# Later and split steps of the attention units, later weight sums, and two more matmuls ahead of router steps in a hybrid decoder layer

## The chip, the cores and the metric

The kernel runs on one core of a Trainium2 chip, in one launch. The metric is the device time of that core in microseconds (us), the median of the runs shown. Inputs, weights and outputs are float32.

## What is computed

One layer for 256 prompt tokens and 8 sample tokens (264 rows, `NT`), model width 1024:

```python
proj = rmsnorm(x) @ w_in                    # xin | Bg | Cg | q | k | v | g_conv | g_attn
y_conv = Bg * causal_depthwise_conv3(Cg * xin)
y_attn = sliding-window GQA(q, k, v), window 128, T5 bias, one sink per head
x = x + (sigmoid(g_conv) * y_conv + sigmoid(g_attn) * y_attn) @ w_out
x = x + MoE(rmsnorm(x))                     # top-4 of 32 experts, clamped SwiGLU
```

The expert weights are 32 x 12.6 MB. Every expert is loaded and computed, in 16 pairs.

## The kernel before

**Stages.** The kernel is written as one program for each engine, with semaphores between them. Three stages follow each other on TensorE (PE): the input projection with the attention (`STEPS`), the output projection with the router (`BRANCH`), and the experts (`pair`). SyncE (SP) issues nearly all weight loads in one queue, in program order, into a ring of six slots and later into four units of two slots; each load waits until PE has begun or finished what was in its place.

**Input projection.** `w_in` comes in 13 chunks (c = 0 to 12) of 512 columns. Of most chunks PE computes four tiles of 128 columns, numbered 0 to 49 over the whole stage; chunk 7 holds tiles 26 to 29 (Cg), chunk 8 tiles 30 to 33 (xin). Chunks 6, 9, 10, 11 and 12 (`SEVEN`) are computed in seven products of half blocks instead of eight, a Strassen form: `slot(c, s)` is product s of chunk c, in `product()` on PE and `seven()` on VectorE (DVE). It needs sums of weights, four DVE instructions for each chunk (`add_weights`, placed by `SUM_STEPS`), and differences of the activations (`sides`, placed by `SIDE_STEPS`). DVE reads the products out of PSUM as r1, w, c22, c12 and c21; ScalarE (ACT) copies the first as t1 and computes the gates' sigmoids in place. PE's product s = 2 waits for t1, s = 6 for c22, and s = 0, 1, 4, 5 of the next chunk for the reads of the one before.

**Attention.** It is done in four units of 4 x 2 heads (`UNITS`): units 0 and 3 are of the first 128 queries, units 1 and 2 of the last 128 and have keys in two blocks. A unit goes through seven steps, whose places among the tiles and slots are in `UNIT_STEPS`: scores (PE), bias and peak (DVE), exp (ACT: eight activations, with a table load where the sigmoid's table was in), norm (for units 1 to 3 a reciprocal on DVE and then eight scalings on ACT), a move of 32 x 32 blocks by DMAs of 32 KB from the GpSimd (POOL) and SP queues into `stage[0]` (in `hn`) and `stage[1]` (`conv_row`), turn (DVE transposes them into `probT`), values (PE, then a DVE copy to `ya`). `plan()` puts each step behind its tile or slot; within one engine the steps stand in that order, and a step that has to wait holds up all that is behind it on that engine.

**What hangs on these steps.** SP issues the moves of units 1, 2 and 3 ahead of the loads of chunks 10, 12 and 13 (`MOVED_BEFORE`). After the loads of `w_out` (chunks 13 and 14) SP waits for the values of unit 3 (`FILL["values", 3]`), issues 12 moves of the expert biases, and then the first expert weights, in the order of `FIRST_ORDER`: pieces 0, 1, 11, 2, 3, 10, 7, 4, 5, 6, 8, 9 of 2 MB. POOL also waits for these values before its 12 moves. The biases are split on ACT and DVE into three bf16 parts (`split`, placed by `SPLIT_STEPS`). `conv_rows` (at `CONV_STEP`) is a DVE transposition; POOL stores its result with eight DMAs and then issues its moves of unit 3.

**Output and router.** `BRANCH` lists the steps for all engines. ("part", (n, k0, k1)) is the product of tokens 128 to 255 with half n of the last 512 columns of `w_out`, k from k0 to k1. ("x_cols", a) transposes new x on PE and copies it to `hT` on DVE (L1274), groups and logits are router products, count the ranks of the chosen experts, ahead the first two products of the last logits.

## Time and profile before

| | |
|---|---|
| runs, us | 1154.15, 1157.01, 1155.16 (median 1155.16) |
| profiled execution, us | 1155.1 |
| its span, us | 1153.2 |
| PE busy, us | 1100.5 (95%) |
| DVE / ACT / POOL busy, us | 440.8 / 183.7 / 82.8 |
| moved by DMA | 444.34 MB, mean 385 GB/s |
| granted TensorE clock | 0.993 of full speed |

The profile is of one execution. Times in the trace count from the start of the span, and 1.9 us of the execution lie outside it. An idle time in brackets is the time that the engine stood still before the instruction, with what released it. PE's instructions are counted twice in float32, since each is done in two passes.

### The profile page before, as it was taken

The page shows a single profiled execution, that of the slowest core. Times are in us where ns is not written, and L with a number is a line of the kernel's source. Part 1 is how long each engine was busy: PE and PEld are TensorE (multiplying, and loading weights), DVE is VectorE, ACT ScalarE, POOL GpSimd, SP SyncE. Part 2 cuts the span into 40 slices and gives each one's busy share as a digit, 9 for nine tenths or more (in the row PEclk, how much of TensorE's full clock was granted, in tenths as well). Part 3 has the DMA queues.
Part 4 walks back from the last instruction along what each step waited for, and adds up shares of the span by engine and source line. Part 5 has one row for each costly group of instructions (what it writes and reads, how often), then busy time and mean ns, then how long its engine had stood idle before and what let it go on. Part 6 is the DMA issues. An engine that isn't in the chain of part 4 may idle for free.

```text
span 1153.2 us, 14712 instructions
## 1 busy us (share of the span) xinstructions
PE 1100.5 (95%) x5895; PEld 494.2 (43%) x5895; DVE 440.8 (38%) x877; ACT 183.7 (16%) x388; POOL 82.8 (7%) x149
## 2 busy tenths in 40 slices
PE   9999999999999999999999999999999999999997
PEld 6678899453333333333333333333333333333332
DVE  4876775752353132332323232323232323232322
ACT  2123331220231111010101010101010101010101
POOL 1775033000000000000000000000000000000000
PEclk9999999999999999999999999999999999999999
DMA  9965439989999999999999999999999999999996
GB/s 318 327 194 130 151 98 300 399 317 431 424 419 426 421 430 429 435 432 430 429 435 433 431 429 435 433 429 431 435 432 429 432 434 432 429 433 434 425 423 280
DMA packets 52819, 444.34 MB, mean 385 GB/s; under 512 B 13036, under 2 KB 19596, under 8 KB 35868
## 3 DMA queue, kind: packets, MB, share of 16 engines
q1 hardware_dynamic: 46712, 436.13, 90.8%
q0 software_dynamic: 5216, 7.03, 2.4%
q10 hardware_dynamic: 852, 0.64, 0.2%
q8 instruction: 28, 0.46, 0.2%
q14 instruction: 11, 0.09, 0.0%
HBM read 439.78 MB, written 2.37 MB: 383 GB/s over the span
## 4 chain that ended last, share of the span: by engine, by line
PE 54%; DMA 38%; POOL 3%; DVE 3%; ACT 1%; issue 1%; SPq 0%; DVEq 0%; ACTq 0%; POOLq 0%
PE pA L1960 29%; DMA ring<-in_w_up 21%; PE pB L1960 18%; DMA ring<-in_w_down 10%; PE pM L1960 6%; DMA area<-in_w_up 5%; PE pM L1963 1%; DMA hn<-in_cache_v_win 1%; POOL keys L952 1%; DMA ring<-in_w_in 1%; PE pA L1963 1%; DMA out<-area 0%; POOL out L960 0%; POOL area L931 0%; POOL conv_row L937 0%
## 5 line engine op out<-in xcount | busy, mean ns | idle before, releaser
L1960 PE MATMUL pA<-ring,hn 128*64 128x512 f32 x1536 | 352.6, 602 | 23.4 <-DMA ring<-in_w_up 23.4
L1960 PEld LDWEIGHTS pA<-ring,hn 128*64 128x64 f32 x1536 | 105.3, 137 | 219.2 <-issue 185.5
L1960 PE MATMUL pB<-ring,area 128*64 128x512 f32 (+2 forms) x784 | 171.5, 591 | 6.6 <-DMA ring<-in_w_down 5.8
L1960 PE MATMUL pB<-area,ring 128*128 128x264 f32 (+2 forms) x928 | 148.5, 350 | 2.2 <-ACT tmp L1080 0.8
L1960 PEld LDWEIGHTS pB<-area,ring 128*128 128x128 f32 (+1 forms) x928 | 120.4, 175 | 27.7 <-issue 4.3
L1960 PE MATMUL pA<-area,hn 128*64 128x512 f32 x512 | 119.3, 609 | 10.4 <-DMA area<-in_w_up 10.4
L1960 PEld LDWEIGHTS pB<-ring,area 128*64 128x64 f32 (+2 forms) x784 | 58.6, 136 | 101.2 <-issue 87.8
L1812 DVE TENSOR_TENSOR x<-pM,x 128x512 f32<-128x512 f32 x60 | 40.1, 692 | 147.3 <-PE pM L1960 147.2
L1183 ACT ACTIVATE area<-area 128x512 f32<-128x512 f32 x30 | 18.9, 631 | 385.2 <-DVE area L1795 385.2
L1727 DVE COPY conv_row<-pM 128x512 f32<-128x512 f32 x30 | 20.6, 686 | 146.4 <-PE pM L1960 146.4
L1960 PEld LDWEIGHTS pA<-area,hn 128*64 128x64 f32 x512 | 36.1, 140 | 74.6 <-issue 59.8
L1960 PE MATMUL pB<-area 128*64 128x512 f32 (+2 forms) x300 | 66.4, 547 | 1.2 <-DVE area L1260 1.2
L1795 DVE TENSOR_SCALAR area<-pA 128x512 f32<-128x512 f32 x30 | 20.7, 691 | 92.6 <-PE pA L1960 92.6
L1960 PE MATMUL pM<-area 128*128 128x512 bf16 (+2 forms) x368 | 52.4, 330 | 1.5 <-DVE x L1812 1.4
L1730 DVE TENSOR_TENSOR hn<-pM,fnorm 128x512 f32<-128x512 f32 x30 | 20.7, 691 | 84.9 <-PE pM L1963 84.5
L1837 DVE COPY area<-pB 64x512 f32<-64x512 f32 x15 | 10.4, 694 | 101.5 <-PE pB L1960 101.5
L1960 PEld LDWEIGHTS pM<-area 128*128 128x128 bf16 (+2 forms) x368 | 18.7, 96 | 52.4 <-issue 35.6
L1960 PE MATMUL pM<-hn,x 128*128 128x512 bf16 (+1 forms) x120 | 37.4, 396 | 0.0
L1960 PEld LDWEIGHTS pB<-area 128*64 128x64 f32 (+2 forms) x300 | 20.7, 130 | 35.0 <-issue 30.3
L1195 ACT ACTIVATE area<-pA 128x512 f32<-128x512 f32 x15 | 9.0, 597 | 120.7 <-PE pA L1963 120.7
L1963 PEld LDWEIGHTS pA<-cst,area 128*128 128x128 f32 x120 | 16.8, 210 | 24.3 <-issue 24.3
L1191 ACT ACTIVATE area<-pA 128x512 f32<-128x512 f32 x15 | 8.9, 596 | 107.0 <-PE pA L1963 107.0
(335 smaller groups left out, 933.9 us busy)
## 6 DMA issues: line engine op xcount, KB each, us to landing
ring<-in_w_up SPq DMA_DIRECT2D x36, 4096.0 KB, 29.8
ring<-in_w_down SPq DMA_DIRECT2D x18, 4096.0 KB, 29.1
area<-in_w_up SPq DMA_DIRECT2D x12, 4096.0 KB, 30.2
ring<-in_w_up SPq DMA_DIRECT2D x17, 2048.0 KB, 14.6
area<-in_w_down SPq DMA_DIRECT2D x6, 4096.0 KB, 30.0
ring<-in_w_in SPq DMA_DIRECT2D x22, 1024.0 KB, 11.2
ring<-in_w_up SPq DMA_DIRECT2D x14, 1024.0 KB, 9.3
ring<-in_w_down SPq DMA_DIRECT2D x13, 1024.0 KB, 25.9
```

Of the source, the lines that this page charges most:

```text
L952: pool.dma_start(v_row[32 * a:32 * a + 32, 0:2, 32 * q:32 * q + 32], v_blocks[32 * q:32 * q + 32].rearrange("p (m a r) -> p m a r", m=2, a ...
L1183: nc.scalar.activation(early_sig if kind == "first" else sig[:, e, :], early_glu if kind == "first" else glu[:, e, :], ACT.Sigmoid, scale= ...
L1191: nc.scalar.activation(turned, pA[:, 0:512], ACT.Copy).then_inc(aT_ready, 1)
L1195: nc.scalar.activation(turned, pA[:, 1024:1536], ACT.Copy).then_inc(aT_ready, 1)
L1727: return V.tensor_copy(xrow[:, 512 * half:512 * half + 512], b)
L1730: return V.tensor_tensor(xsT[:, 4 * half:4 * half + 4, :], b.rearrange("p (k s) -> p k s", k=4), fw[:, 4 * half:4 * half + 4, :], ALU.mult)
L1795: V.tensor_scalar(gl, u[:, 0, e], LIMIT, None, ALU.min).then_inc(glu_ready, 1)
L1812: V.tensor_tensor(xo, bank(k), xo, ALU.add).then_inc(misc_free, 1)
L1837: V.tensor_copy(y_pair[64:128, 512:1024], pB[64:128, 1, :]).then_inc(y_ready_dve, 1)
L1960: return pe.matmul(out, w, m, start=start, stop=stop, skip_group_check=True)
L1963: return pe.transpose(out, src, ident[0:src.shape[0], 0:src.shape[0]])
```

## The change

Four tables are changed.

- `UNIT_STEPS`: exp and norm of unit 1 stand one tile earlier, its turn four steps earlier and its values one tile earlier. Bias, peak and exp of unit 2 stand one tile earlier, its turn and values one slot later. Unit 3's turn goes from slot (10, 6) to (11, 1), its values from (11, 1) to (11, 3).
- The turn of units 1 and 2 is split: the transposition of `stage[0]` stays at the turn, that of `stage[1]` stands at a step of its own (`SECOND_TURNS`).
- `SUM_STEPS` of chunks 9 and 10, the last of `SIDE_STEPS`, `SPLIT_STEPS` and `CONV_STEP` are placed anew. Since the last side is now computed behind slot (9, 0), chunk 9 uses `side3[0]` like chunk 6, and only the chunks in `AFTER_XIN` (10, 11, 12) use `side3[1]`.
- `BRANCH`: one more k of part 0 ahead of groups, and one more k of part 1 ahead of count 0.

The diff also adds a case for a Cg chunk in the seven-product form. `SEVEN` holds no such chunk, so this case adds no instruction; it is left out below.

```diff
-UNIT_STEPS = [(11, 12, 12, 13, 13, 18, 19), (18, 18, 19, 20, 21, 27, 28),
-              (26, 27, 28, 29, 30, slot(9, 2), slot(9, 4)),
-              (slot(9, 3), slot(9, 4), slot(9, 5), slot(10, 0), slot(10, 2), slot(10, 6), slot(11, 1))]
-SPLIT_STEPS = [slot(9, 4), slot(9, 6), slot(10, 1)]
-CONV_STEP = slot(10, 1)
-SIDE_STEPS = [20, 21, slot(6, 2), slot(6, 3), 33]
-SUM_STEPS = {6: (19, 20, slot(6, 0), slot(6, 1)), 9: (slot(6, 5), 26, 26, 28), 10: (29, 29, 30, 31),
+UNIT_STEPS = [(11, 12, 12, 13, 13, 18, 19),
+              (18, 18, 19, 19, 20, slot(6, 5), 27),
+              (26, 26, 27, 28, 30, slot(9, 3), slot(9, 5)),
+              (slot(9, 3), slot(9, 4), slot(9, 5), slot(10, 0), slot(10, 2), slot(11, 1), slot(11, 3))]
+SECOND_TURNS = (26, slot(9, 3))
+SPLIT_STEPS = [slot(9, 6), slot(10, 1), slot(10, 4)]
+CONV_STEP = slot(10, 2)
+SIDE_STEPS = [20, 21, slot(6, 2), slot(6, 3), slot(9, 0)]
+SUM_STEPS = {6: (19, 20, slot(6, 0), slot(6, 1)),
+             9: (slot(6, 4), 27, 28, 29),
+             10: (30, 31, slot(9, 0), slot(9, 1)),
              11: (slot(10, 0), slot(10, 1), slot(10, 3), slot(10, 4)),
              12: (slot(11, 2), slot(11, 3), slot(12, 1), slot(12, 2))}
...
+    for n, step in enumerate(SECOND_TURNS):
+        after[step].append(("turn", len(UNITS) + 1 + n))
...
+          ("s_split", 0), ("out", (1, 0)), ("x_cols", 2), ("rms", 0), ("part", (0, 0, 6)), ("groups", 0), ("x_cols", 3),
+          ("logits", 0), ("part", (0, 6, KT)), ("half", 0), ("part", (1, 0, 4)), ("count", 0), ("part", (1, 4, 6)),
...
-            gated = TILES[2 + 4 * (c - 1)][0] != "bg"
+            kind = TILES[2 + 4 * (c - 1)][0]
+            gated = kind in ("gc", "ga")
-                if name != "c11" or not gated:
+                if name != "c11" or kind == "bg":
-                if name == "t1" or gated:
+                if name == "t1" or gated or name == "c11" and kind == "cg":
...
+AFTER_XIN = [c for c in SEVEN if STEPS.index(("slot", (c, 0))) > STEPS.index(("sides", 4))]
...
-                elif what == "turn":
+                elif what == "turn" and a < len(UNITS):
                     dve.wait_ge(prob_moved, MOVED[a])
                     if SYNC_MOVED[a]:
                         dve.wait_ge(moved_by_sync, SYNC_MOVED[a])
-                    for b in range(UNITS[a][0] + 1):
-                        ins = V.transpose(probT[:, b].rearrange("p h q -> p (h q)"), stage[b])
-                    ins.then_inc(probT_ready, 1)
+                    ins = V.transpose(probT[:, 0].rearrange("p h q -> p (h q)"), stage[0])
+                    if UNITS[a][0] == 0:
+                        ins.then_inc(probT_ready, 1)
+                elif what == "turn":
+                    V.transpose(probT[:, 1].rearrange("p h q -> p (h q)"), stage[1]).then_inc(probT_ready, 1)
...
-                                  (s1, side1, bank_y, False), (s3, side3[c > SEVEN[0]], bank_u, True), (s4, b22, bank_v, True),
+                                  (s1, side1, bank_y, False), (s3, side3[c in AFTER_XIN], bank_u, True), (s4, b22, bank_v, True),
...
-                    pe.wait_ge(h_ready, KT + (3 if c == SEVEN[0] else 5))
-                    if opening:
+                    pe.wait_ge(h_ready, KT + (5 if c in AFTER_XIN else 3))
+                    if UNITS_BEFORE[c]:
                         pe.wait_ge(prob_biased, UNITS_BEFORE[c])
-                    else:
+                    if not opening:
```

**The norm of unit 1.** On DVE, around the last two tiles of chunk 5 (`area<-pB 128x264`), before. The two `stat` rows are the norm of unit 1 (wait `exp_done`), the `ring` rows weight sums of chunk 6, the `128x528` rows sides.

```order
L1384 TENSOR_TENSOR area<-area 128x528
L1371 TENSOR_TENSOR ring<-ring 128x1024 [waits sums_ready]
L1453 TENSOR_TENSOR area<-pB,area 128x264 [waits tile_full]
L1384 TENSOR_TENSOR area<-area 128x528 [waits h_ready]
L1541 TENSOR_TENSOR stat<-stat 128x8 [waits exp_done]
L1543 RECIPROCAL stat<-stat 128x8 [waits dve_step]
L1371 TENSOR_TENSOR ring<-ring 128x1024
L1312 TENSOR_TENSOR tmp<-tmp,pB 128x264 [waits tile_free_act,tile_full]
```

And in the changed kernel:

```order
L1401 TENSOR_TENSOR area<-area 128x528
L1388 TENSOR_TENSOR ring<-ring 128x1024 [waits sums_ready]
L1558 TENSOR_TENSOR stat<-stat 128x8 [waits exp_done]
L1560 RECIPROCAL stat<-stat 128x8 [waits dve_step]
L1470 TENSOR_TENSOR area<-pB,area 128x264 [waits tile_full]
L1401 TENSOR_TENSOR area<-area 128x528 [waits h_ready]
L1388 TENSOR_TENSOR ring<-ring 128x1024
L1324 TENSOR_TENSOR tmp<-tmp,pB 128x264 [waits tile_free_act,tile_full]
```

The norm now stands ahead of the read of tile 21, behind the sums of step 20, where it stood behind that read and a side.

**The turn of unit 3.** On DVE, end of chunk 10 and start of chunk 11, before. `STREAM_TRANSPOSE` is the turn, `area<-pM` the copy of the values, `tmp` and `rt` from `pB` are r1 and w of chunk 11, the `ring` rows sums of chunk 12.

```order
L1555 STREAM_TRANSPOSE area<-hn 128x1024 [waits moved_by_sync,prob_moved]
L1298 TENSOR_TENSOR area<-tmp,area 128x2x132 [waits tile_free_dve,tile_free_act]
L1312 TENSOR_TENSOR tmp<-tmp,pB 128x264 [waits sig_used,tile_free_act,tile_full]
L1561 COPY area<-pM 128x2x2x128 [waits misc_full]
L1371 TENSOR_TENSOR ring<-ring 128x1024 [waits ring_free,ring_full2]
L1312 TENSOR_TENSOR rt<-tmp,pB 128x264 [waits tile_full]
L1371 TENSOR_TENSOR ring<-ring 128x1024 [waits sums_ready]
```

And in the changed kernel:

```order
L1309 TENSOR_TENSOR area<-tmp,area 128x2x132 [waits tile_free_dve,tile_free_act]
L1324 TENSOR_TENSOR tmp<-tmp,pB 128x264 [waits sig_used,tile_free_act,tile_full]
L1571 STREAM_TRANSPOSE area<-hn 128x1024 [waits moved_by_sync,prob_moved]
L1388 TENSOR_TENSOR ring<-ring 128x1024 [waits ring_free,ring_full2]
L1324 TENSOR_TENSOR rt<-tmp,pB 128x264 [waits tile_full]
L1388 TENSOR_TENSOR ring<-ring 128x1024 [waits sums_ready]
L1580 COPY area<-pM 128x2x2x128 [waits misc_full]
```

The turn is behind the last gate of chunk 10 and r1 of chunk 11, and the copy of the values is behind w and two sums instead of ahead of them.

**The router steps.** On PE, from the first part of half 0 to the transposition of x_cols 4, before. The rows from `ring,area` with `128x256` are the parts, `32x128` is groups, `mask` is count 0.

```order
L1960 MATMUL pA<-ring,area 128x256 x5
L1960 MATMUL pM<-area,router 32x128 [waits wr_ready,misc_free]
L1960 MATMUL pM<-area,router 32x128 x7
L1963 MATMUL pM<-cst,x 128x128 [waits x_added,misc_free]
L1963 MATMUL pM<-cst,x 128x128 x3
L1960 MATMUL pM<-cst,sprobT 128x32 [waits misc_free]
L1960 MATMUL pA<-ring,area 128x256 x3
L1960 MATMUL pB<-ring,area 128x256 x3
L1960 MATMUL pM<-mask,router 8x32 [waits mask_ready,misc_free]
L1960 MATMUL pM<-mask,router 128x32 x2
L1960 MATMUL pB<-ring,area 128x256 x3
L1963 MATMUL pM<-cst,x 128x128 [waits x_added,misc_free]
L1963 MATMUL pM<-cst,x 128x128
```

And in the changed kernel:

```order
L1979 MATMUL pA<-ring,area 128x256 x6
L1979 MATMUL pM<-area,router 32x128 [waits wr_ready,misc_free]
L1979 MATMUL pM<-area,router 32x128 x7
L1982 MATMUL pM<-cst,x 128x128 [waits x_added,misc_free]
L1982 MATMUL pM<-cst,x 128x128 x3
L1979 MATMUL pM<-cst,sprobT 128x32 [waits misc_free]
L1979 MATMUL pA<-ring,area 128x256 x2
L1979 MATMUL pB<-ring,area 128x256 x4
L1979 MATMUL pM<-mask,router 8x32 [waits mask_ready,misc_free]
L1979 MATMUL pM<-mask,router 128x32 x2
L1979 MATMUL pB<-ring,area 128x256 x2
```

Six matmuls instead of five stand ahead of groups, and two instead of three behind count 0.

## Rows read from the trace of the kernel before

**Rows 1.** Busy time by stretch; columns as in the second line.
```profile
core 0: us, PE busy (x) PEld busy (x) DVE busy (x) ACT busy (x) POOL busy (x), PEclk, DMA share, GB/s
75.00:210.00 135.00, 133.65 (x1054) 115.74 (x1055) 95.66 (x198) 34.66 (x110) 41.51 (x74) 1.00 0.57 178
210.00:247.00 37.00, 35.72 (x177) 22.14 (x177) 23.61 (x78) 12.12 (x27) 0.00 (x0) 1.00 0.84 342
247.00:512.00 265.00, 262.35 (x1280) 93.58 (x1278) 88.31 (x180) 41.01 (x64) 0.00 (x0) 1.00 1.00 424
512.00:1136.00 624.00, 584.39 (x2827) 209.90 (x2827) 180.40 (x308) 73.30 (x120) 0.00 (x0) 0.99 1.00 431
```

**Rows 2.** PE in order of time: start, length, idle before.
```profile
105.82 3.87 PE L1960 MATMUL pB<-area,ring 128*128 128x132 f32 x32 [0.82 <-ACT tmp L1080]
...
118.58 1.32 PE L1960 MATMUL pA<-keys,area 64*32 64x160 f32 x64
...
179.47 1.08 PE L1960 MATMUL pM<-area,keys 128*64 128x256 f32 x8 [0.22 <-issue]
...
228.96 2.32 PE L1960 MATMUL pA<-ring,area 128*128 128x256 f32 x10
...
231.67 0.65 PE L1960 MATMUL pM<-area,router 128*32 128x128 f32 x16 [0.38 <-DVE area L1274]
```

**Rows 3.** ScalarE in order of time, 95 to 169 us.
```profile
95.55 0.43 ACT L1095 ACTIVATE area<-area,stat 128x160 f32<-128x160 f32 x1 [22.21 <-DVE stat L1536]
...
98.85 0.19 ACT L1097 ACTIVATE stat<-stat 128x8 f32<-128x8 f32 x1
...
102.83 2.66 ACT L1102 ACTIVATE area<-area,stat 128x160 f32<-128x160 f32 x8 [3.79 <-DVE stat L1543]
...
133.29 1.28 ACT L1095 ACT_TABLE_LOAD   x1
...
168.36 0.62 ACT L1110 ACTIVATE conv_row<-hn 128x512 bf16<-128x512 f32 x1
```

**Rows 4.** VectorE in order of time.
```profile
99.14 1.22 DVE L1371 TENSOR_TENSOR ring<-ring 128x1024 f32<-128x1024 f32 x1
...
121.32 1.52 DVE L1521 SCALAR_TENSOR_TENSOR area<-pA,area 128x640 f32<-128x640 f32 x2
...
178.13 1.25 DVE L1555 STREAM_TRANSPOSE area<-hn 128x1024 f32<-128x1024 f32 x1 [1.32 <-DMA hn<-area]
...
230.89 0.68 DVE L1274 COPY area<-pM 128x512 f32<-128x512 f32 x1
```

**Rows 5.** GpSimd's DMA issues in order of time.
```profile
169.18 0.59 POOL L991 DMA_DIRECT2D out<-hn  x1 [19.79 <-DVE hn L1598]
...
173.68 2.91 POOL L971 DMA_DIRECT2D hn<-area  x5
```

**Rows 6.** SyncE's DMA issues in order of time.
```profile
176.64 2.36 SPq L740 DMA_DIRECT2D ring<-in_w_out  x4
...
181.32 0.87 SPq L747 DMA_DIRECT2D keys<-conv_row  x1
...
190.16 1.05 SPq L821 DMA_DIRECT2D ring<-in_w_up  x2
...
228.83 10.35 SPq L821 DMA_DIRECT2D ring<-in_w_up  x2
```

**Rows 7.** The two gaps of the DMA engines; columns as in rows 1.
```profile
228.00:231.00 3.00, 3.00 (x16) 2.29 (x14) 2.92 (x6) 0.00 (x0) 0.00 (x0) 1.00 0.50 131
...
235.00:239.00 4.00, 4.00 (x23) 3.18 (x22) 2.64 (x13) 0.51 (x2) 0.00 (x0) 1.00 0.03 12
```

**Rows 8.** DMA issues from 160 to 262 us: KB each, median us to landing.
```profile
keys<-conv_row SPq DMA_DIRECT2D x6, 32.0 KB, 8.5
...
keys<-conv_row POOLq DMA_DIRECT2D x6, 32.0 KB, 5.7
...
hn<-area POOLq DMA_DIRECT2D x5, 32.0 KB, 1.9
```

More of the change, by code:

```diff
@@ L248 @@
 BRANCH = [("out", (2, 0)), ("out", (0, 0)), ("x_cols", 0), ("rms", 2), ("out", (0, 1)), ("x_cols", 1), ("logits", 2),
-          ("s_split", 0), ("out", (1, 0)), ("x_cols", 2), ("rms", 0), ("part", (0, 0, 5)), ("groups", 0), ("x_cols", 3),
-          ("logits", 0), ("part", (0, 5, KT)), ("half", 0), ("part", (1, 0, 3)), ("count", 0), ("part", (1, 3, 6)),
+          ("s_split", 0), ("out", (1, 0)), ("x_cols", 2), ("rms", 0), ("part", (0, 0, 6)), ("groups", 0), ("x_cols", 3),
+          ("logits", 0), ("part", (0, 6, KT)), ("half", 0), ("part", (1, 0, 4)), ("count", 0), ("part", (1, 4, 6)),
           ("x_cols", 4), ("part", (1, 6, KT)), ("half", 1), ("ahead", 1), ("x_cols", 5), ("rms", 1), ("logits", 1),
@@ L1080, in _ @@
                         nc.scalar.activation(t1, pairs_of(bank_x), ACT.Copy).then_inc(tile_free_act, 1)
+                    elif s == 2 and (c, "c11") in ACT_DONE and not gated:
+                        act.wait_ge(tile_full, FULL[c, 2])
+                        nc.scalar.activation(quarter(cx[:, :, 2:], c, "c11"), pairs_of(bank_x), ACT.Copy).then_inc(tile_free_act, 1)
                     elif s == 2 and gated:
@@ L1309, in seven, with place_of @@
                 gated = (c, "c22") in ACT_DONE
+                plain = TILES[2 + 4 * (c - 1)][0] == "cg"
                 def read(name, out, a, b):
                     V.tensor_tensor(out, a, pairs_of(b), ALU.add).then_inc(tile_free_dve, 1)
+                def place_of(name, g):
+                    return quarter(cx[:, :, 2:], c, name) if plain else g
                 def times(name, g):
+                    if plain:
+                        return
                     dve.wait_ge(tile_free_dve, DVE_READ[c, name])
@@ L1322, in seven @@
                     return
-                if s != 2 or not gated:
+                if s != 2 or not (gated or plain):
                     dve.wait_ge(tile_full, FULL[c, s])
@@ L1329, in seven @@
                     read("r1", r1, t1, bank_y)
-                elif s == 2 and not gated:
+                elif s == 2 and not (gated or plain):
                     out = quarter(yc, c, "c11")
@@ L1336, in seven @@
                     dve.wait_ge(tile_free_dve, DVE_READ[c, "w"])
-                    read("c22", c_, w_, bank_u)
+                    read("c22", place_of("c22", c_), w_, bank_u)
                     if not gated:
@@ L1340, in seven @@
                 elif s == 5:
-                    read("c12", w_, w_, bank_v)
+                    read("c12", place_of("c12", w_), w_, bank_v)
                     if gated:
@@ L1348, in seven @@
                         finish(c, "c12")
-                    read("c21", r1, r1, bank_u)
+                    read("c21", place_of("c21", r1), r1, bank_u)
                     if not gated:
```

## The prediction

> **What bounds the kernel now.** I read the busy time by stretch first, since PE is busy for 95% of the span and that figure alone tells nothing. Up to 210 us PE stands still for 135.00 - 133.65 = 1.4 us after 75 us while the DMA engines are busy for 0.57 of the time; from 210 to 247 us it stands still for another 1.3 us. From 512 us on it is the other way round: PE is idle for 40 of 624 us and the DMA share is 1.00 [rows 1]. Between 247 and 512 us both are full. So the end is set by the stream of expert weights, at about 430 GB/s, and that stream starts when PE frees its places. A microsecond saved ahead of 247 us reaches the end only if it lets that stream go on earlier; a microsecond by which an issue of SP slips costs only if the stream has no gap left to swallow it.
>
> The gaps are in the windows of the stream: a half-idle stretch from 228 to 231 us, and one with a share of 0.03 from 235 to 239 us [rows 7]. Together they are 1.5 + 3.9 = **5.4 us** of idle DMA time. Both end when PE has got far enough in the router: SP issues the next pieces at 228.83 us and then ten microseconds later [rows 6].
>
> Then I read PE in order of time, for its idle before an instruction, and from there to the engine named. Three places lie where the change works [rows 2]: 0.82 us ahead of product s = 2 of chunk 6 (waiting for t1 on ACT), 0.22 us ahead of the values of unit 3, and 0.38 us ahead of groups (waiting for DVE's copy of x_cols 2). All of PE's idle time from 75 to 247 us is 2.6 us, so nothing that the change does there can bring more than that. PE's work stays the same, matmul for matmul.
>
> **The change part by part.**
>
> *Norm of unit 1, one tile earlier.* Its exps end at 98.85 + 0.19 = 99.0 us [rows 3]. In the new order the norm stands behind a weight sum that ends at 100.3 us [rows 4], and no longer behind the read of tile 21. Reciprocal and its companion need some 0.3 us, so the eight scalings (2.66 us) start at about 100.7 us instead of 102.83 and end at 103.3 instead of 105.5. Product s = 0 of chunk 6 ends about 1.8 us before 105.0, where PE became ready, thus at 103.2 (a slot takes 3.7 / 2 = 1.8 us [rows 2]). t1 is then written by 103.8, and PE needs it at 105.0. The whole **0.82 us** goes. What is late next is r1 for s = 3, which follows on time.
>
> *Turn and values of unit 1.* The moves now start at 103.4 us. Ten on SP take 6.8 us to issue at the 0.6 to 0.7 us each that its other rows show, the last lands about 2 us later [rows 8], so near 112.3. The turn stands behind slot (6, 5), at 113.2. If it had to wait, c21 would be read later, and PE needs that only ahead of the scores of unit 2, at 118.58 - 0.8 = 117.8 us [rows 2]: cover of over 2 us. The second transposition follows bias 2, so 119.1 + 1.5 + 1.2 = 121.8 us [rows 4], and PE asks for it one tile (3.6 us) behind the end of these scores at 119.1, at 122.7. Cost nothing, with 0.9 us in hand.
>
> *Exp of unit 2 ahead of the copy of tile 29 on ACT.* Table load 1.28, exps 3.5, two copies 0.8 [rows 3]: 5.6 us behind the end of tile 28. PE wants that bank for tile 31, two tiles or 7.2 us behind it. Nothing, with 1.6 us in hand.
>
> *Sums and the last side.* The same instructions, on DVE, which is 0.71 busy [rows 1]. Sums of chunk 10 end behind slot (9, 1), a whole chunk ahead of use. Nothing.
>
> *Splits and conv_rows.* The second cast now runs on ACT behind the exps of unit 3, where the third ran at 168.36 us [rows 3]. With PE 0.8 us earlier that cast ends at 168.5. DVE then subtracts (about 1.0 us, two instructions of the cast's shapes), does the norm of unit 3 and transposes. POOL's stores therefore start at about 170.6 instead of 169.18 us [rows 5], its moves of unit 3 at 175.1 instead of 173.68, and these are issued by 178.1. Behind the waiting subtraction stand w and c22 of chunk 10; PE needs c22 at about 172.9 us and has it at 172.1. Nothing on PE, but a margin of 0.8 us.
>
> *Turn and values of unit 3, later.* Before, DVE waited 1.32 us for the moves and PE 0.22 us for the turn [rows 4, 2]. Now PE has two more slots to do: it comes to the values at 179.25 - 0.82 + 3.6 = 182.05 us. The moves land at 179.5 (the last issued at 177.5, plus 1.9 [rows 8]) and the turn is done at 180.8. So the **0.22 us** goes too. The copy of the values now follows w and two sums; it ends at about 184.3, where it ended at 181.3. SP's bias moves (8.8 us of issuing), and behind them the expert weights, start **3.0 us later**: at 193.2 instead of 190.16 us [rows 6]. The stream before was unbroken from there to 228 us, so its first seven pieces now end at about 231.2. The piece issued at 228.83 - 1.2 us then ends at 236.1, and the next is issued, with PE earlier by 1.4, at 237.4. The 5.4 us of gap shrink by 3.0 + 1.4 to 1.0 us. Cost nothing while that is left; beyond it each microsecond counts in full.
>
> *Router.* Five matmuls take 2.32 us, one 0.46 [rows 2]. The sixth covers the 0.38 us of waiting (DVE's copy, at 230.89 us [rows 4], hangs on a chain that moves with PE). Groups start 0.08 us later than they could, but 0.46 us less of part work stands behind count 0, whose other inputs move with PE. From there to the last logits the path is shorter by **0.38 us**.
>
> Sum: 0.82 + 0.22 + 0.38 = 1.42 us, passed on to the stream because its later pieces are gated by PE. The profiled execution took 1155.1 us (span 1153.2 and 1.9 around it), 0.06 below the median, so the forecast is 1155.1 - 1.4 = **1153.7 us**. Bounds of the sum: all of PE's idle time gone, -2.6 us; nothing gained, 0.
>
> **The rivals.**
>
> *A: the moves of unit 3 land late.* On POOL they are now issued until 178.1 us, while SP, freed 0.8 us earlier, issues `w_out` from 175.8 us on. Before, POOL was done at 176.6, when `w_out` began [rows 5, 6]. In the quiet such a move lands in 1.9 us, beside heavy loads one of 32 KB took 5.7 us on POOL and 8.5 on SP [rows 8]. At 5.7 the last lands at 183.2, the turn is done at 184.5, and PE stands still for 2.5 us; SP's issue slips by 6.5 us, which the gap of 5.4 + 2.5 - 1.4 just swallows. The time is 1155.1 - 1.4 + 2.5 = 1156.2 us, slower than before. At 8.5 it would be 1159.0. It decides from a landing above 3.1 us. For it: the two queues now overlap by 2 us. Against it: the loads of `w_out` moved few bytes in their first 2 us. The Trainium skill ("DMA: Bandwidth & Descriptors", section "Queues, rings and completion order") says that each DMA engine takes turns between the queues at packet granularity, and that a completion write lands only after every earlier write of that engine, whichever queue it is from. By that rule the late case is the natural one, for a move issued behind bulk work; no run here shows it for these moves.
>
> *B: the saving does not reach the stream.* If the copy of the values slips by 1 us more than I reckon, the gap is gone and PE's 1.4 us are eaten by waits later: 1155.1 us, no change. For it: only 1.0 us is left. Against it: the window before was measured, not guessed.
>
> *C: a wait takes the place of t1's.* One of the margins of 0.8 or 0.9 us (c22 of chunk 10, second turn of unit 1) is not there, and PE loses up to 1 us: 1154.7.
>
> A gain over 0.3% would need 3.5 us, more than PE's idle time there.
>
> **How the numbers follow.** Forecast 0.52, A 0.25 (of it 0.06 beyond 1158.6), B 0.13, C 0.10. A measurement tells a difference from none from about 0.3%, 3.5 us. All but the end of A lies within; for the spread of the runs (1154.15 to 1157.01) I leave 0.06 for faster. Range: below the forecast 1.2 us for the rest of the idle time and 0.5 for the spread, 1152.0; above, A at 5.7 us and 0.7 for the spread, 1156.9.
>
> **What would show it.** In the changed profile: no idle ahead of s = 2 of chunk 6, of the values of unit 3, and of groups; SP's first expert piece at about 193 us; a DMA gap before 239 us of about 1 us in place of 5.4; pair 0's first matmul 1.4 us earlier. A DVE wait at the turn of unit 3 of over 2 us with PE idle behind it means A; a DMA share of 1.00 through 225 to 240 us means B. I am wrong if PE's idle time from 75 to 247 us grows.

## The result, and the profile after

| | before | changed |
|---|---|---|
| runs side by side, us | 1155.6 median of 13 (1154.15 to 1157.01) | 1159.3 median of 13 (1155.86 to 1161.56) |
| ratio | | 1.003, 95% interval 1.0022 to 1.0039 |
| profiled execution, its span, us | 1155.1, 1153.2 | 1158.37, 1156.3 |

The forecast was 1153.7 us. The changed kernel is slower, by 3.7 us in the medians, and its runs spread over 5.7 us where those of before spread over 2.9. The time lies above the range, and past the 1156.2 us of rival A, near its far end of 1159.0.

Where the time went is seen first in the windows of the changed kernel (the columns are those of [rows 1]).

```profile
core 0: us, PE busy (x) PEld busy (x) DVE busy (x) ACT busy (x) POOL busy (x), PEclk, DMA share, GB/s
75.00:210.00 135.00, 131.90 (x1047) 115.25 (x1048) 92.61 (x194) 33.99 (x109) 41.52 (x74) 0.99 0.51 163
210.00:247.00 37.00, 36.28 (x172) 21.81 (x172) 25.04 (x78) 12.00 (x25) 0.00 (x0) 1.00 0.89 367
```

Up to 210 us PE now stands still for 135.00 - 131.90 = 3.1 us, against 1.4 [rows 1]; with the 0.7 us up to 247 it is 3.8 against 2.6. That is the sign named beforehand ("I am wrong if PE's idle time from 75 to 247 us grows"). PE in order of time shows that two of the three waits of [rows 2] are gone and the third has grown:

```profile
99.79 8.92 PE L1979 MATMUL pB<-area,ring 128*128 128x264 f32 x71
...
117.60 1.32 PE L1979 MATMUL pA<-keys,area 64*32 64x160 f32 x64
...
184.69 1.98 PE L1979 MATMUL pM<-area,keys 128*64 128x256 f32 x8 [2.81 <-issue]
186.59 4.39 PE L1979 MATMUL pA<-area,ring 128*128 128x132 f32 x32
...
234.69 0.65 PE L1979 MATMUL pM<-area,router 128*32 128x128 f32 x16
...
249.42 2.80 PE L1979 MATMUL pA<-ring,hn 128*64 128x512 f32 x12
```

The product that followed 0.82 us of idle runs on without a stop (99.79 to 108.7 is one row), and groups at 234.69 has no idle time before it. But PE stands still for 2.81 us ahead of the values of unit 3, where it was 0.22. The view names no releaser there (`issue`); the turn that PE needs ends at 183.34 + 1.25 = 184.6 us by VectorE's row further down, 0.1 us before PE goes on. The values themselves then take 1.98 us instead of 1.08, and the first two products behind them 4.39 instead of 3.87 us. The windows of this stretch tell why (the granted clock is the third number from the end):

```profile
183.00:185.00 2.00, 0.31 (x2) 0.32 (x4) 1.66 (x2) 0.00 (x0) 0.00 (x0) 0.82 1.04 384
185.00:187.00 2.00, 2.00 (x10) 0.94 (x7) 2.00 (x3) 0.00 (x0) 0.00 (x0) 0.50 1.06 389
187.00:189.00 2.00, 2.00 (x16) 2.00 (x16) 0.77 (x2) 0.00 (x0) 0.94 (x2) 0.83 1.05 386
```

The granted clock was 0.50 from 185 to 187 us, that is 1.2 in place of 2.4 GHz, right behind the 2.81 us in which PE did nothing. Before, it was 1.00 throughout this stage [rows 1].

From PE I went to VectorE, which does the norm and the turns, and from there to the moves: four views of the changed kernel, VectorE, POOL's and SP's issues in order of time, and the DMA issues from 160 to 262 us with KB each and the median us to landing.

```profile
100.59 0.20 DVE L1560 RECIPROCAL stat<-stat 128x8 f32<-128x8 f32 x1
...
120.62 1.25 DVE L1575 STREAM_TRANSPOSE area<-conv_row 128x1024 f32<-128x1024 f32 x1
...
183.34 1.25 DVE L1571 STREAM_TRANSPOSE area<-hn 128x1024 f32<-128x1024 f32 x1 [4.60 <-DMA hn<-area]
```

```profile
170.28 0.59 POOL L999 DMA_DIRECT2D out<-hn  x1 [21.87 <-DVE hn L1617]
...
174.78 2.91 POOL L979 DMA_DIRECT2D hn<-area  x5
```

```profile
175.67 2.54 SPq L748 DMA_DIRECT2D ring<-in_w_out  x4
```

```profile
hn<-area SPq DMA_DIRECT2D x5, 32.0 KB, 2.0
hn<-area POOLq DMA_DIRECT2D x5, 32.0 KB, 4.8
...
out<-hn POOLq DMA_DIRECT2D x4, 8.0 KB, 1.8
```

POOL's stores and moves are issued as forecast (170.28 and 174.78 us; 170.6 and 175.1 were reckoned), the last move starts at about 177.1 and is issued by 177.7. But the median landing of POOL's five is 4.8 us, where it was 1.9 [rows 8], and the turn waits 4.60 us, until 183.34. SP's five, issued just before `w_out`, land in 2.0. Between the two stands one event: at 175.67 SP begins to issue `w_out`. Its bytes come later, as two windows of the changed kernel show (the last number is GB/s):

```profile
177.00:178.00 1.00, 1.00 (x11) 1.00 (x10) 0.00 (x0) 0.00 (x0) 0.69 (x2) 1.00 0.31 43
178.00:179.00 1.00, 1.00 (x11) 1.00 (x10) 0.43 (x1) 0.00 (x0) 0.00 (x0) 1.00 1.02 387
```

PE's first matmul of the experts starts at 249.42 us. Before, in the same place of the program, it was

```profile
246.84 3.65 PE L1960 MATMUL pA<-ring,hn 128*64 128x512 f32 x16
```

Of the 3.27 us between the profiled executions 2.58 are there at that point; the rest is within the spread of the runs. The profiled execution of the changed kernel, 1158.37 us, lies 0.9 below its median, so it holds only part of the loss of 3.7.

### The profile page after: what moved, and what is told of

It is laid out like the page before. It is cut to its first block, busy times and chain, and to the rows that moved or that the text cites. A ratio compares the mean times of both kernels' runs of the same rounds, so it can differ in the third digit from the quotient of the medians.

```text
span 1156.3 us, 14714 instructions
## 1 busy us (share of the span) xinstructions
PE 1102.3 (95%) x5895; PEld 495.1 (43%) x5895; DVE 440.7 (38%) x877; ACT 183.3 (16%) x388; POOL 82.8 (7%) x149
## 4 chain that ended last, share of the span: by engine, by line
PE 55%; DMA 38%; POOL 3%; DVE 2%; ACT 1%; issue 1%; SPq 0%; DVEq 0%; ACTq 0%; POOLq 0%
PE pA L1979 29%; PE pB L1979 19%; DMA ring<-in_w_up 16%; DMA ring<-in_w_down 12%; DMA area<-in_w_up 8%; PE pM L1979 6%; PE pM L1982 1%; DMA hn<-in_cache_v_win 1%; POOL keys L960 1%; DMA ring<-in_w_in 1%; PE pA L1982 1%; DMA out<-area 0%; POOL out L968 0%; POOL area L939 0%; POOL conv_row L945 0%
```

## The experiments

Two theories stood against each other. **L**: the moves of unit 3 land late because `w_out` is under way beside them, and the loss is PE's idle time, with the slow clock behind it. **S**: the loss comes from SP's slip, since the stream of expert weights starts later. Every kernel ran in turn with the kernel before on one chip, and each ratio is against it.

### 1. The moves ahead of the stores

```diff
             move_blocks(2)
+            move_blocks(3)
             pool.wait_ge(blocks_turned, CONV_TURNED)
             for q in range(4):
...
-            move_blocks(3)
```

> The changed kernel, but POOL issues its five moves of unit 3 ahead of the eight stores of conv_rows. Theory L (the moves of unit 3 land late because POOL issues them beside the load of w_out, and PE loses its idle time and then its clock): the last POOL move is issued near 175 us and lands within about 2 us; no DVE wait of over 0.5 us at the turn of unit 3, no PE idle ahead of the values of unit 3, granted clock 1.00 there, first expert matmul near 245.5 us; time 1.2 to 1.6 us below the kernel before, near 1154.2. Rival S (the later start of the expert stream is the cost, 3.0 us of it by the place of the values alone): SP's first expert piece still comes near 193 us and the time stays within 1 us of the changed kernel, near 1158.5.

**Measured: 1153.86 us** (1152.62 to 1155.25, 11 runs), ratio 0.9986 (0.9977 to 0.9995). DMA issues from 160 to 262 us (KB each, median us to landing), then PE in order of time:

```profile
hn<-area POOLq DMA_DIRECT2D x5, 32.0 KB, 1.9
...
out<-hn POOLq DMA_DIRECT2D x4, 8.0 KB, 5.7
```

```profile
181.78 1.08 PE L1979 MATMUL pM<-area,keys 128*64 128x256 f32 x8
182.79 3.87 PE L1979 MATMUL pA<-area,ring 128*128 128x132 f32 x32
...
245.11 3.65 PE L1979 MATMUL pA<-ring,hn 128*64 128x512 f32 x16
```

The two landings show L in the plainest way. The five moves, now issued from 172.60 us, land in 1.9 us; the stores, now issued last and beside `w_out`, land late in their place: those of 8 KB in 5.7 us, where they took 1.8. Nobody waits for them. In these runs moves and stores alike land late when POOL issues them behind the first load of `w_out`. PE has no idle time ahead of the values, they take 1.08 us again, and the experts' first matmul comes at 245.11, 1.73 us earlier than before and 4.31 earlier than in the changed kernel.

### 2. conv_rows and the splits earlier

```diff
-SPLIT_STEPS = [slot(9, 6), slot(10, 1), slot(10, 4)]
-CONV_STEP = slot(10, 2)
+SPLIT_STEPS = [slot(9, 5), slot(9, 6), slot(10, 1)]
+CONV_STEP = slot(10, 1)
```

> The changed kernel with the splits at (9, 5), (9, 6), (10, 1) and conv_rows at (10, 1), so that POOL's stores and its moves of unit 3 come about 2 us earlier while the order on POOL stays. Theory L: POOL's last move is issued near 175.5 us, lands before 178, no PE idle ahead of the values; time as moves_first, near 1154.2. Rival S: near 1158.5. If the long landing were of the moves themselves and not of the overlap with w_out, the DVE wait at the turn stays above 3 us here and in moves_first.

**Measured: 1153.32 us** (1152.85 to 1154.73, 11 runs), ratio 0.9981 (0.9972 to 0.9990). The moves are issued from 173.40 us and land in 1.8; PE does not stop at the values.

### 3. w_out held back

```diff
                 if c in MOVED_BEFORE:
                     move_blocks(MOVED_BEFORE[c])
+                if c == W_IN_CHUNKS:
+                    sp.wait_ge(prob_moved, MOVED[3])
                 if before(c):
                     sp.wait_ge(ring_free, before(c))
```

The wait stands in SP's loop over the chunks, ahead of the loads of chunk 13, the first of `w_out`.

> The changed kernel with one more wait on SP: the load of w_out is issued only when POOL's moves of unit 3 have landed. Theory L: these moves land 2 us after their issue (1.7 to 2.3) although POOL issues them as late as in the changed kernel, until about 177.7; landing near 179.5, DVE's wait at the turn about 1 us, no PE idle ahead of the values; w_out starts 4 us later and is still there before PE needs it near 201 us; the expert stream starts near 193 us; time near 1154.5. If POOL's moves are slow by themselves: landing still 5 us and more, PE idle as in the changed kernel, time near 1159.

**Measured: 1153.67 us** (1152.9 to 1154.48, 11 runs), ratio 0.9982 (0.9973 to 0.9991). This one keeps POOL's order and times and takes only the bulk away. POOL's and SP's issues in order of time, and the landing:

```profile
174.72 2.90 POOL L981 DMA_DIRECT2D hn<-area  x5
```

```profile
178.87 2.14 SPq L750 DMA_DIRECT2D ring<-in_w_out  x4
```

```profile
hn<-area POOLq DMA_DIRECT2D x5, 32.0 KB, 1.8
```

Issued at 174.72 to 177.6, as late as in the changed kernel, the moves land in 1.8 us. So the cause is not the late issue in itself but the load beside it.

### 4. The kernel before, with conv_rows late

```diff
-SPLIT_STEPS = [slot(9, 4), slot(9, 6), slot(10, 1)]
-CONV_STEP = slot(10, 1)
+SPLIT_STEPS = [slot(9, 6), slot(10, 1), slot(10, 4)]
+CONV_STEP = slot(10, 2)
```

> The kernel before with only the places of the splits and of conv_rows changed to those of the change. Theory L: this part alone brings the loss. POOL's moves of unit 3 are issued until about 178 us, beside w_out (issued from 176.6); the turn, which here stands one slot earlier, waits 3 to 6 us on DVE, PE stands still 2 to 5 us ahead of a product of chunk 11 or the values, and its clock falls to half for some 2 to 3 us: time 1158 to 1162. Rival S: the turn and the values have the old places, so the stream starts late only by the wait; without a wait the time is that of the kernel before, 1155.6.

**Measured: 1164.05 us** (1163.12 to 1164.76, 5 runs), ratio 1.0075 (1.0061 to 1.0088). PE and VectorE of this kernel in order of time, and its windows:

```profile
185.04 1.98 PE L1960 MATMUL pM<-area,keys 128*64 128x256 f32 x8 [6.31 <-issue]
186.95 5.04 PE L1960 MATMUL pB<-area,ring 128*128 128x132 f32 x32
```

```profile
183.69 1.25 DVE L1555 STREAM_TRANSPOSE area<-hn 128x1024 f32<-128x1024 f32 x1 [7.41 <-DMA hn<-area]
```

```profile
183.00:185.00 2.00, 0.00 (x0) 0.00 (x0) 1.31 (x2) 0.00 (x0) 0.00 (x0) 0.50 1.05 369
...
187.00:189.00 2.00, 2.00 (x10) 2.00 (x10) 1.82 (x2) 0.00 (x0) 0.96 (x2) 0.50 1.09 395
189.00:193.00 4.00, 4.00 (x36) 4.00 (x35) 0.98 (x2) 0.39 (x1) 3.67 (x9) 0.95 0.47 146
```

The two-line edit alone makes the loss. Idle time grew by 6.31 - 0.22 = 6.1 us, and at half the clock the values and the two products behind them took (1.98 - 1.08) + (5.04 - 3.87) = 2.1 us more. Together 8.2, against 1164.05 - 1155.76 = 8.3 measured, above the 1158 to 1162 that I had expected. Profile against profile, PE comes to the experts 254.46 - 246.84 = 7.6 us later and the execution is 1163.12 - 1155.10 = 8.0 us longer. What PE loses here reaches the end nearly one for one.

### 5 and 6. Only the stream held back

```diff
             sp.wait_ge(misc_free, FILL["values", 3])
             sp.wait_ge(bias_cast, SPLITS)
+            sp.wait_ge(tile_full, FULL[11, 5])
```

This is the kernel of experiment 1 with one more wait on SP: in the first run, `stream_held`, for product 5 of chunk 11, in the second, `stream_held_longer`, for product 0 of chunk 12 (`FULL[12, 0]`).

> The kernel moves_first, and in addition SP waits for product s = 5 of chunk 11 ahead of the bias moves. PE has nothing more to wait for; the stream of expert weights alone is held back. In moves_first the copy of the values ended at 183.4 us and the first expert piece was issued at 191.98; product 5 ends at about 190.3, so that piece should be issued at about 199, 7 us later. Idle DMA time from 228 to 239 us in moves_first was 3.00 * 0.06 + 4.00 * 0.20 + 4.00 * 0.69 = 3.7 us. If a slip is swallowed by that gap and counts in full beyond it, 3.3 us are left over: 1153.9 + 3.3 = 1157.2 us, and no idle DMA time from 228 to 239 us. If the slip costs nothing because the later pieces are gated by PE: 1153.9. If it costs in full from the start: 1160.9.

> As stream_held, but SP waits for product s = 0 of chunk 12, which ends at about 190.1 us (a product takes 1.8 to 1.9 us). In stream_held the first expert piece was issued at 194.44 us, 2.46 later than in moves_first, and of the idle DMA time from 228 to 239 us 1.4 us (4.00 * 0.36) was left, at no cost in time. Now the piece should be issued at about 198.1, another 3.7 us later. If the gap swallows what it holds and the rest counts in full: 3.7 - 1.4 = 2.3 us, so 1153.8 + 2.3 = 1156.1 us, a DMA share near 1.00 from 228 to 239 us. If slips cost nothing: 1153.8.

**Measured: 1153.80 us** (1153.12 to 1154.91, 11 runs) and **1153.81 us** (1152.67 to 1154.57, 11 runs), both with the ratio 0.9985 (0.9976 to 0.9994). The first expectation had the end of product 5 wrong (186.4 and not 190.3 us, since a product takes half of what I took for it), so it tested a slip of 2.5 us; the second tested 198.09 - 191.98 = 6.1. SP's issues and the windows of the second kernel:

```profile
198.09 1.05 SPq L830 DMA_DIRECT2D ring<-in_w_up  x2
...
226.95 9.94 SPq L830 DMA_DIRECT2D ring<-in_w_up  x2
```

```profile
228.00:231.00 3.00, 3.00 (x30) 2.20 (x28) 2.33 (x8) 1.52 (x4) 0.00 (x0) 1.00 1.03 437
...
235.00:239.00 4.00, 3.78 (x28) 3.36 (x27) 2.52 (x12) 1.15 (x4) 0.00 (x0) 1.00 0.96 410
```

The first expert piece is issued at 198.09 us, 7.9 us later than before [rows 6], the gaps of [rows 7] are all but full, and the time is that of experiment 1. That is later than in the changed kernel itself:

```profile
196.45 1.05 SPq L829 DMA_DIRECT2D ring<-in_w_up  x2
```

So the slip of the stream doesn't make the loss. S is refuted for slips as long as this one, and with it the arithmetic by which 1.0 us was left. Part of the error is the unit: the DMA share counts an engine as busy while it moves little. In experiment 1 the windows read

```profile
228.00:231.00 3.00, 3.00 (x29) 2.24 (x27) 2.59 (x8) 0.93 (x4) 0.00 (x0) 1.00 0.94 322
231.00:235.00 4.00, 4.00 (x25) 3.24 (x23) 2.92 (x14) 1.65 (x3) 0.00 (x0) 1.00 0.80 336
235.00:239.00 4.00, 3.78 (x28) 3.34 (x27) 2.68 (x13) 0.71 (x3) 0.00 (x0) 1.00 0.31 66
```

By the shares 0.18 + 0.80 + 2.76 = 3.7 us are free there; by the bytes, against 430 GB/s, 0.8 + 0.9 + 3.4 = 5.0 us. The slip of 6.1 us is still 1 us longer than that, and what took up this last microsecond stays open. Where a slip begins to cost was not tried.

### 7. The values one product later

```diff
-              ... slot(10, 2), slot(11, 1), slot(11, 3))]
+              ... slot(10, 2), slot(11, 1), slot(11, 4))]
```

> The changed kernel with the values of unit 3 one product later still, behind slot (11, 4). The moves of unit 3 are issued as late as in the changed kernel, and should land as late (median near 4.8 us), but PE now does another product of 3.8 us ahead of the values, so it comes there at about 185.6 us, when the turn is done at 184.6. Theory L (all the loss is PE's idle time and the half clock behind it): no idle ahead of the values, granted clock 1.00, time 1153.9. Theory S (the late start of the stream costs too): first expert piece at about 197 us, 5 us later than in moves_first, against a gap of 3.7: 1153.9 + 1.3 = 1155.2.

**Measured: 1155.06 us** (1153.53 to 1156.23, 11 runs), ratio 0.9996 (0.9987 to 1.0005). A product takes 1.9 us, not the 3.8 that I had written, so the wait should shrink by 1.9 and not vanish. PE in order of time, and the landing:

```profile
183.89 1.08 PE L1979 MATMUL pM<-area,keys 128*64 128x256 f32 x8 [0.84 <-issue]
```

```profile
hn<-area POOLq DMA_DIRECT2D x5, 32.0 KB, 5.0
```

It shrank from 2.81 to 0.84 us, the moves landed as late as before (5.0), and after an idle time of 0.84 us the values took 1.08 us: the clock did not fall. The median is 1.2 us above experiment 1. The profiled execution, 1153.53 us, is the shortest of the eleven, so its 0.84 us do not measure what the others lost. The median lies near the 1155.2 that I had given to S, but the first expert piece came at 195.42 us here, and 198.09 cost nothing in experiment 6. That leaves PE's remaining wait as the likely reason; in the longer executions it was not traced.

### 8. The router steps alone, in the kernel before

```diff
-          ... ("part", (0, 0, 5)), ("groups", 0), ("x_cols", 3),
-          ("logits", 0), ("part", (0, 5, KT)), ("half", 0), ("part", (1, 0, 3)), ("count", 0), ("part", (1, 3, 6)),
+          ... ("part", (0, 0, 6)), ("groups", 0), ("x_cols", 3),
+          ("logits", 0), ("part", (0, 6, KT)), ("half", 0), ("part", (1, 0, 4)), ("count", 0), ("part", (1, 4, 6)),
```

> The kernel before with the new order of the router steps alone. The term of the sum says -0.38 us: no idle ahead of groups, 1155.8 - 0.4 = 1155.4. If the work moved there is missed behind count 0, a new idle time of up to 0.46 us stands there and the time is that of before, 1155.8.

**Measured: 1155.15 us** (1154.24 to 1155.85, 11 runs; the kernel before 1155.65 beside it), ratio 0.9994 (0.9985 to 1.0003). The medians differ by 0.5 us, the size of the term, but the interval takes in no change. In the trace the idle time ahead of groups is gone and no new one stands behind it.

### 9. Units 1 and 2 alone

The changed kernel with unit 3, the splits, `conv_rows` and the router steps as before:

```diff
-              (... slot(10, 0), slot(10, 2), slot(11, 1), slot(11, 3))]
+              (... slot(10, 0), slot(10, 2), slot(10, 6), slot(11, 1))]
-SPLIT_STEPS = [slot(9, 6), slot(10, 1), slot(10, 4)]
-CONV_STEP = slot(10, 2)
+SPLIT_STEPS = [slot(9, 4), slot(9, 6), slot(10, 1)]
+CONV_STEP = slot(10, 1)
```

> The changed kernel with unit 3, splits, conv_rows and the router steps as before: only the steps of units 1 and 2, the sums and the last side are new. The term of the sum says -0.82 us (no idle ahead of product s = 2 of chunk 6), 1155.8 - 0.8 = 1155.0; moves of unit 3 issued before w_out as in the kernel before, landing in about 1.9 us. PE comes to the values of unit 3 earlier by 0.8, so that part of the 0.82 can come back there as a wait where the chain of unit 3 hangs on POOL or ACT and not on PE: then 0.22 + 0.8 = 1.0 us of idle ahead of the values and 1155.8. If this part brought the loss, it would be over 1157.

**Measured: 1154.64 us** (1153.63 to 1154.84, 11 runs; before 1155.65), ratio 0.9990 (0.9981 to 0.9999). A gain of 1.0 us (0.1 to 2.2 by the interval) for a term of 0.82. PE's waits of this kernel between 95 and 235 us are one:

```profile
230.12 0.65 PE L1979 MATMUL pM<-area,router 128*32 128x128 f32 x16 [0.38 <-DVE area L1285]
```

It is the 0.38 us ahead of groups, which this kernel keeps. Nothing came back at the values of unit 3.

### 10. The idle time filled with work

```diff
                     o = misc_bank()
+                    if a == 3:
+                        for n in range(12):
+                            matmul(o[:, 0:HALF], weights(11)[0][:, n % K2, 0:128], b11[:, n % K2, :])
                     pe.wait_ge(probT_ready, a + 1)
```

> The changed kernel with 12 more matmuls of 128x132 on PE ahead of its wait for the turn of unit 3; their result is overwritten by the values. At 0.235 us each (3.76 us for 16) they fill 2.8 us, as long as PE stood still there in the profiled execution of the changed kernel. They change no transfer and nothing on VectorE. If the stretch at half the clock is brought about by the idle time: granted clock 1.00 from 183 to 189 us, the values 1.08 us again in place of 1.98 and the product behind them 3.76 in place of 4.39, so 1.5 us less: 1159.3 - 1.5 = 1157.8. If the clock fell for another cause: still 0.50 there and 1159.3. In both cases DVE still waits over 3 us for the moves.

**Measured: 1156.34 us** (1155.81 to 1158.10, 11 runs), ratio 1.0012 (1.0002 to 1.0021). PE in order of time, a window, and VectorE:

```profile
181.24 2.86 PE L1979 MATMUL pM<-area,ring 128*128 128x132 f32 x24
185.62 1.08 PE L1979 MATMUL pM<-area,keys 128*64 128x256 f32 x8 [1.52 <-DVE area L1571]
186.63 3.87 PE L1979 MATMUL pA<-area,ring 128*128 128x132 f32 x32
```

```profile
185.00:187.00 2.00, 1.38 (x11) 0.85 (x12) 2.00 (x4) 0.00 (x0) 0.00 (x0) 1.00 1.06 388
```

```profile
184.32 1.25 DVE L1571 STREAM_TRANSPOSE area<-hn 128x1024 f32<-128x1024 f32 x1 [6.05 <-DMA hn<-area]
```

The trace has two records for each float32 matmul, so x24 is the twelve. In this execution the moves landed later still (the turn waited 6.05 us), and PE spent 2.86 us on the filling and 1.52 idle. The clock stays at 1.00, the values take 1.08 and the products behind them 3.87 us. Part of the loss is thus the slow clock and not the wait. In the profiled execution of the changed kernel it cost (1.98 - 1.08) + (4.39 - 3.87) = 1.4 us. The two profiled executions themselves are only 0.3 us apart (1158.37 and 1158.10, here the longest of the eleven): PE began the values 0.9 us later, at 185.62 against 184.69. The medians, 1159.3 and 1156.34, differ by 3.0, twice the 1.4 and more than the 1.5 expected. The runs here stand in two groups, six from 1155.81 to 1156.34 and five from 1157.57 to 1158.10, as if the landing had two values, the earlier one hidden by the filling; that is a guess, since only one execution of each kernel was traced. How late the moves landed, and what the clock cost, in those executions of the changed kernel that took over 1160 us stays open too.

### 11 and 12. Both mendings together

The edit of experiment 2 on top of experiment 1, and on top of experiment 3.

> The changed kernel with both mendings: conv_rows and the splits at steps (9, 5), (9, 6), (10, 1), (10, 1), and the moves of unit 3 ahead of POOL's stores. Either alone took away all idle time ahead of the values (1153.86 and 1153.32), so the second should add nothing: 1153.3 to 1153.9, moves issued from about 170 us and landing in 1.9, SP's first expert piece at 191.9. If the earlier start of the stream were worth something, up to 0.6 us less than moves_first: 1153.2.

> The changed kernel with conv_rows and the splits early, and w_out held until the moves of unit 3 have landed. In conv_early these moves landed in 1.8 us with w_out beside them, so holding w_out should change nothing but its issue, at about 177.5 us in place of 175.7: 1153.3. If the spread of landing from run to run were left in conv_early, this kernel would be lower or spread less than 1152.85 to 1154.73.

**Measured: 1153.57 us** (1152.63 to 1155.07, 11 runs), ratio 0.9987 (0.9978 to 0.9996), and **1153.31 us** (1152.77 to 1153.96, 11 runs), ratio 0.9980 (0.9971 to 0.9989). As expected, once PE's wait is gone there is nothing left for a second mending. Only the issue was not as expected: with both mendings the moves start at 172.32 us and not at about 170, since POOL waits for unit 3's scalings on ACT. Experiment 2 changes only two lines and is 2.4 us below the kernel before, 6.0 below the changed one; the intervals do not tell it from experiments 1 and 3.

What the landings have in common, row by row (the first column of times runs from the start of the first issue to the end of the last; the clock is that of the values):

| kernel | POOL issues the moves | SP issues `w_out` from | landing, median us | clock behind |
|---|---|---|---|---|
| before | 173.68 to 176.6 | 176.64 | 1.9 | 1.00 |
| moves_first | 172.60 to 175.5 | 175.63 | 1.9 | 1.00 |
| conv_early | 173.40 to 176.3 | 176.26 | 1.8 | 1.00 |
| w_out_held | 174.72 to 177.6 | 178.87 | 1.8 | 1.00 |
| changed | 174.78 to 177.7 | 175.67 | 4.8 | 0.50 |
| before_conv_late | 175.21 to 178.1 | 176.10 | 4.8 | 0.50 |
| values_later | 174.13 to 177.0 | 175.02 | 5.0 | 1.00 |
| idle_filled | 174.31 to 177.2 | 175.19 | 4.8 | 1.00 |

In the kernel before, the last move was issued just as the first load of `w_out` began (176.6 and 176.64), and in `conv_early` too. Wherever POOL's issues ran on for 2.0 us beyond that, the moves landed late. Between these two cases nothing was tried, so how much overlap is harmless stays open.

## Why the prediction was wrong

**The step that failed** is in the part on unit 3: "The moves land at 179.5 (the last issued at 177.5, plus 1.9 [rows 8])". The issue was right to 0.4 us; the landing was a figure from the quiet, used for five moves of which three were now issued behind the first load of `w_out`. They landed at about 183.3. Experiments 1 and 3 show it from two sides, one by moving the moves, one by taking `w_out` away. The case stood there as rival A, with its rule, and I gave it 0.25. My reason against it was that `w_out` moved few bytes in its first 2 us. It was no reason: the last move, issued at 177.1, would have landed at 179.0 in the quiet, and the bulk of `w_out` was there from 178 us on (43 GB/s up to 178 us, 387 behind it). The Trainium skill ("DMA: Bandwidth & Descriptors", section "Queues, rings and completion order") says that an engine takes turns between queues and that a completion write lands only after every earlier write of that engine. The trace agrees with the effect (4.8 against 1.8 us, and the stores' 5.7 against 1.8 when they take the moves' place); which of the two parts of the rule does it no run here tells apart.

**A's price was too low.** At a landing of 5.7 us it reckoned 2.5 us of idle PE and 1156.2 us. The idle time was 2.81, but the half clock behind it had no term: 1.4 us in the profiled execution, 2.1 in experiment 4. Together PE came 4.3 us later to the experts than in experiment 1. The forecast had none of these 2.81 + 1.4 = 4.2 us; the median missed it by 5.6, and the 1.4 us between are not explained; 0.9 of them is what the median lies above the profiled execution. A's slip of SP's issue does not come out of its own terms either: 3.0 + 2.5 is 5.5 and not 6.5 us. That 196.45 - 190.16 = 6.3 were measured is luck.

**The three gains were right.** The 0.82 us went (experiment 9: 1.0 measured), the 0.38 too (experiment 8: 0.5, not certain), and with the moves in time the 0.22 as well. The kernels of the whole change in which the moves land in time took 1153.3 to 1153.9 us, about the forecast's 1153.7. In part that is luck: the kernel before took 1155.5 to 1155.8 beside them and not the 1155.1 from which I had reckoned, so they gained 1.7 to 2.4 us for a sum of 1.4. PE's gain in experiment 1 is 246.84 - 245.11 = 1.7 us.

**The margins held.** The turn of unit 1 went from step 27 to slot (6, 5), which is three steps and not four, and it did not wait. The reciprocal ahead of the scalings of unit 1 starts at 100.59 and they at 100.83 (100.7 us reckoned), the second transposition ends at 120.62 + 1.25 = 121.9 (121.8), and no wait took t1's place: C did not come.

**The margin of the stream was wrong in the other direction.** "Beyond it each microsecond counts in full" was stated for 1.0 us left of 5.4. A first piece 7.9 us later than before cost nothing (experiment 6). In the changed kernel itself, with its first piece at 196.45, the DMA share from 235 to 239 us was 0.82, so even there the gap was not used up. Rival B had its 0.13 from that arithmetic and was not there. What did reach the end was the time by which PE came late to the experts. Against the profile of before it is 7.6 us of 8.0 in experiment 4 and 2.6 of 3.3 in the changed kernel. The second is rough, since executions of one kernel differ by over 2 us: against experiment 1, whose profiled execution (1155.25) is the longest of its eleven, it is 4.3 us of PE for 3.1 in time.

## What to carry to other kernels

Take the landing time of a small transfer from a row in which the same neighbours are under way, not from the quiet; if two queues come to overlap, move the small one ahead of the bulk or hold the bulk, either for nothing here. A wait of some microseconds on TensorE can cost more than itself: look at the granted clock of the rows behind it, and price it in. And before a slip of a stream is counted, hold the stream back alone and see: a gap that looks used up may not be.

## What the runs showed of the hardware

- A DMA of 32 KB or less on GpSimd's queue landed in 1.7 to 2.1 us (median) when it was issued before the first of the 1 MB loads on SP's queue or with that load held back, and in 4.8 to 5.7 us when most of its group was issued behind the first of them, whether move or store.
- After 2.81 and 6.31 us without a matmul the granted clock was 0.50 (1.2 GHz) for the next instructions, and it was back at 1.00 some microseconds after PE had gone on (in the changed kernel from 188 to 189 us); after 0.84 us, and after 1.52 us behind twelve matmuls of filling, it stayed at 1.00. I had counted on an idle time costing its own length only. The Trainium skill ("TensorE: Matmul & The Clock Gate", section "Part 1: The HAM clock gate (the "warmup" mystery)") says that the lower clock is the idle engine's and that activity lifts it; these rows agree.
- The DMA share is no measure of what is left: 228 to 231 us had a share of 0.94 at 322 GB/s in experiment 1 and of 1.03 at 437 in experiment 6.
